# A two-block transformer kernel on one core: dummy products of the identity at stage openings, and a conv FFN whose taps are handed over side by side

## Chip, cores and metric

The kernel runs on one core of a Trainium2 chip. The metric is device time in microseconds (us). Three runs of the kernel before gave 2916.37 to 2916.70 us, median 2916.45.

## The reference

One program computes two stacks of depth 2 on 256 tokens of width 1024, in fp32.

- First stack: an RWKV-7 layer (projections, low-rank gates, the WKV recurrence over 256 steps, group norm, output projection), post-norm, a dense SwiGLU FFN (hidden 2816), post-norm; then causal attention with 16 heads (one MoBA block of 256 keys, so all keys before the query), its output projection, and a mixture of 8 experts of which each token takes 2 (hidden 3584).
- Second stack, on the 256 tokens and 256 context tokens: a layer with neighbourhood attention and a two-way mLSTM side by side, an output projection and a conv FFN on 512 tokens; then multi-head latent attention of the 256 tokens over all 512 keys, its output projection, and a conv FFN on 256 tokens.

The conv FFN is the part whose order changes:

```python
def conv_ffn(h, w_up, conv_w, conv_b, w_down):
    u = dwconv_centred(h @ w_up, conv_w, conv_b)     # 3 taps over the positions, per channel
    a, g = jnp.split(u, 2, axis=-1)
    return (a * jax.nn.silu(g)) @ w_down
```

## The kernel before

The program is a sequence of stages (`K.begin()`), each with a hand-written instruction list for every engine and a barrier between one stage and the next. All weights stream through `weight_ring`, six chunks of 128 x 2048 fp32 (1 MB), loaded by SyncE in the order of a plan; a chunk is loaded as soon as its place is used up (`K.used`).

**Products in two parts.** fp32 accuracy comes from splitting each operand into a rounded part (`high`, fp32r) and the rest (`low`); a product is three fp32r matmuls (high x low, low x high, high x high) that accumulate in PSUM. `class Split` does this for the streamed weights by halves of a chunk (1024 columns): ScalarE (ACT) copies the half into `w_high` (line 265), VectorE (DVE) subtracts it into `w_low` (line 300). In stages that stream x along (`rows`), the same is done for x (`s_x_high` L264, `s_x_low` L298). `depth` 1 keeps two halves, so that a half is split again as soon as PE has used it; `depth` 2 keeps four.

**Openings.** At the start of a stage `act_open` (L275 to L282) splits the first weight half in two pieces, and PE begins with the high x high products of that half (`opening()`: L517 in `linear_rows`, L710 in `gated_ffn`, L386 in `split_cols`, L1860 in `moba_projections`), while DVE makes the first `w_low` and `x_low`. Then PE goes on with the other two parts of the half (L526, L731, L407, L1879).

**gated_ffn.** 11 chunk pairs: for each chunk c a weight chunk for side s=0 (the gated side) and one for s=1, 256 hidden channels each, result in PSUM banks `c % 2 * 4 + s * 2 + h`. Without a convolution ACT applies SiLU to side 0 and DVE multiplies by side 1 (L809). With one, for each c:

- ACT, once both sides are done, writes the centre tap and bias of both (L792, four instructions) and later the SiLU of the chunk before (L767);
- DVE adds the left and right taps of both sides in one go (L832, eight instructions of 128 x 510 in the 512-token FFN), signals `tapped` once, and multiplies the chunk before (L809), before it makes the next `w_low`;
- PE may overwrite the banks of c when `tapped` says that both sides are done. After the last chunk it goes on to the down products (L700), of which the token tiles 0 and 1 take the banks of the last chunk.

The 512-token FFN (depth 1) stands at 2146 to 2530 us of the profile, the 256-token one (depth 2) from 2720 us on.

**WKV.** `wkv` solves triangular systems by levels, two blocks of 128 steps. At its end PE waits for DVE's last masked copy (`dn_at(1,6,1)`, L1578), then makes the last solution (`solved(1, g)`, L1365) and the outputs (`output(1, g)`, L1365 and L1370); DVE copies the outputs (L1595) and normalises them, which ends the stage. PE meanwhile makes conditioning products (L1153).

**attention** (causal, neighbourhood, latent) runs scores (L1724, masks or bias L1731), DVE's maximum (L1801), ACT's exponential (L1820), transposes (L1743), DVE's copy (L1789), the product with v (L1768) and the spreading of sums (L1753), software-pipelined over steps.

**latent** makes the compressed keys and queries of the latent attention, beginning with 64 matmuls (L3531).

`K.ident` is the 128 x 128 identity in fp32, used for transposes. PSUM bank 7 is `K.ps[7]`.

Of the kernel before, what the change touches and what calls it, by code (L numbers as in the profile page):

```python
# [21 lines left out]
P = 128  # L22
D = 1024
KT = D // P
T = 256
TT = T // P
# [339 lines left out]
def split_cols(K, x, jobs, late, parts_at, x_at, extra, kept, small):  # L366
# [11 lines left out]
    with K.begin() as block:  # L378
        @block.tensor
        def _(pe):  # L380
            def opening():
                for h in range(2):
                    for k in range(KT // 2):
                        if h == 0 and k % 2 == 0:
                            pe.wait_ge(*xsplit.at(k // 2 + 1))
                        nc.tensor.matmul(bank(0, h), parts.hi[:, 0, k * 256 + h * P:k * 256 + h * P + P],  # L386
                                         xhi[:, k, :], start=(k == 0), stop=False)

            extra.tensor(pe, 0)
            for c in range(chunks):  # L390
                if c == 1:
                    extra.tensor(pe, extra.pairs)
                if c >= 3:
                    pe.wait_ge(*evac.at(c - 2))
                for i in range(2):
                    opened = c == i == 0
                    if opened:
                        opening()
                    pe.wait_ge(*parts.low.at(2 * c + i + 1))
                    for h in range(2):  # L400
                        for k in range(KT // 2):
                            j = i * (KT // 2) + k
                            if c == h == 0 and j % 2 == 0:
                                pe.wait_ge(*xlow.at(j // 2 + 1))
                            at = slice(k * 256 + h * P, k * 256 + h * P + P)
                            for p, (ws, xs) in enumerate(((parts.lo, xhi), (parts.hi, xlo), (parts.hi, xhi))[0:2 if opened else 3]):
                                last = nc.tensor.matmul(bank(c, h), ws[:, i, at], xs[:, j, :],  # L407
                                                        start=(j == 0 and p == 0 and not opened), stop=(j == KT - 1 and p == 2))
                    last.then_inc(*(K.used if i else parts.half).up())
                K.taken += 1  # L410
# [63 lines left out]

def last_steps(tts, depth):

# [14 lines left out]
def linear_rows(K, x, kts, evac, tts=TT, after=None, sqrts=None, root_bufs=(), depth=2, loads=(), tail=None):  # L492
# [4 lines left out]
    chunks = len(kts) // 2  # L497
    opened = K.begun["opened"]
    opened.base = opened.n
    with ExitStack() as st:  # L500
# [4 lines left out]
        with K.begin() as block:  # L505
            @block.tensor
            def _(pe):
                if not depth:
                    mm_rows(K, pe, x, kts, banks=tuple(range(8)), tts=tts)
                    return  # L510
                def opening():
                    pe.wait_ge(*opened.at(1))
# [142 lines left out]
def gated_ffn(K, x, hid, chunks, over, tail, conv=None, late=None, base=0):  # L655
# [18 lines left out]
    with ExitStack() as st:  # L674
# [13 lines left out]

        read = tapped if conv else free
        with K.begin() as block:  # L690
            @block.tensor
            def _(pe):
# [12 lines left out]
                def opening():  # L705
                    for h in range(2):
                        for k in range(KT // 2):
                            if h == 0 and k % 2 == 0:
                                pe.wait_ge(*xsplit.at(k // 2 + 1))
                            nc.tensor.matmul(bank(0, 0, h), parts.hi[:, 0, k * 256 + h * P:k * 256 + h * P + P],  # L710
                                             xhi[:, k, :], start=(k == 0), stop=False)

                for c in range(chunks):
                    if c >= 2:
                        pe.wait_ge(*read.at(c - 1))
                    for s in range(2):
                        for i in range(2):
                            opened = c == s == i == 0
# [16 lines left out]
                early = range(2, tts) if tts > TT else range(tts)  # L735
                pe.wait_ge(*read.at(chunks - 1))
                for i in range(2):
# [4 lines left out]
                if tts > TT:  # L742
                    pe.wait_ge(*read.at(chunks))
                    for i in range(2):
                        products(0, i, range(TT)).then_inc(*(K.used if i else parts.half).up())
                K.taken += 1
# [11 lines left out]
                K.taken += 1  # L758
                pe.wait_ge(*read.at(chunks))
                tail[0](pe)  # L760

            @block.scalar
            def _(act):
                def silu(c):
                    act.wait_ge(*tapped.at(c + 1))
                    for h in range(2):
                        last = nc.scalar.activation(side[:, c % 2, 0, h, :], side[:, c % 2, 0, h, :], ACT.Silu)  # L767
                    last.then_inc(*gated.up())
# [7 lines left out]
                for c in range(chunks):  # L776
                    parts.act(act, 2 * c + 1 if conv else 2 * c)
                    if conv is None:
                        act.wait_ge(*K.used.at(2 * c + 1))
                        if c >= 2:  # L780
# [4 lines left out]
                        continue  # L785
                    act.wait_ge(*K.used.at(2 * c + 2))
                    if c >= 2:
                        act.wait_ge(*free.at(c - 1))
                    for s in range(2):
                        for h in range(2):  # L790
                            j = (chunks * 2 if s == 0 else 0) + 2 * c + h
                            last = nc.scalar.activation(side[:, c % 2, s, h, :], bank(c, s, h), ACT.Identity,  # L792
                                                        bias=conv[1][:, j:j + 1], scale=conv[0][:, j, 1:2])
                    last.then_inc(*centre.up())
                    if c >= 1:
                        silu(c - 1)
                if conv is not None:
                    silu(chunks - 1)
                for c in range(down):
# [4 lines left out]
            def _(dve):  # L804
# [12 lines left out]
                for c in range(chunks):  # L817
                    parts.dve(dve, 2 * c + 1 if conv or c < chunks - 1 else 2 * c)
                    if conv is None:
                        dve.wait_ge(*K.used.at(2 * c + 2))  # L820
                        product(c)
                        if late and 1 <= c < 5:
                            late(dve, c - 1)
                        continue
                    dve.wait_ge(*centre.at(c + 1))
                    for tap, (dst, src) in enumerate(((slice(1, T), slice(0, T - 1)), (slice(0, T - 1), slice(1, T)))):
                        for s in range(2):
                            for h in range(2):
# [4 lines left out]
                                                                      ALU.mult, ALU.add)  # L833
                        K.v(dve, last, tapped if tap else None)
                    if c >= 1:
                        product(c - 1)
                if conv is not None:
                    product(chunks - 1)
                for c in range(down):
# [472 lines left out]
def wkv(K, AR, Bt, Kt, vr, G0, G1, G2, G3, Dm, DTs, Wm, tri, level, Brow, Krow, Sbd, dstate, bones, yr, gr, bonus, gg, gb, small):  # L1312
# [27 lines left out]
    with K.begin() as block:  # L1340
        @block.tensor
        def _(pe):
# [101 lines left out]
            for c in range(2):  # L1444
# [30 lines left out]
                for g in range(2):  # L1475
# [5 lines left out]
                    up(last, "d_made")  # L1481
                filler(c, 6, 0)
            pe.wait_ge(*dn_at(1, 6, 1))
            for g in range(2):
# [203 lines left out]
def attention(K, st, units, outs, room=None):  # L1688
# [26 lines left out]
    with K.begin() as block:  # L1715
        @block.tensor
        def _(pe):
# [39 lines left out]
            def apply(s):  # L1757
# [12 lines left out]
                last.then_inc(*applied.up())  # L1770

            for s in range(NS + 3):
                if s < NS:
# [62 lines left out]
def moba_projections(K, x, jobs, vr, late, rounded):  # L1836
# [9 lines left out]
    with ExitStack() as st:  # L1846
# [5 lines left out]
        with K.begin() as block:  # L1852
            @block.tensor
            def _(pe):
                def opening():
                    for h in range(2):
                        for k in range(KT // 2):
                            if h == 0 and k % 2 == 0:
                                pe.wait_ge(*xsplit.at(k // 2 + 1))
                            nc.tensor.matmul(bank(0, h), parts.hi[:, 0, k * 256 + h * P:k * 256 + h * P + P],  # L1860
                                             xhi[:, k, :], start=(k == 0), stop=False)

                for c in range(wide):
                    if c >= 3:
# [1605 lines left out]
def latent(K, st, hT, wkv, wq, ups, ckvT, cqT, kT, qT, vr, H, QK):  # L3470
# [34 lines left out]
    with K.begin() as block:  # L3505
        @block.tensor
        def _(pe):
# [14 lines left out]
            def values(n):  # L3522
# [3 lines left out]
                                 start=True, stop=True).then_inc(*value.up())  # L3526

            pe.wait_ge(*K.load.now())
            for tt in range(4):
# [401 lines left out]
```

## Time and profile before

| | us |
|---|---|
| median of 3 runs | 2916.45 |
| the profiled execution, its own time | 2922.09 |
| its span, first to last instruction | 2920.3 |
| TensorE (PE) busy | 2767.4 (95%) |
| VectorE (DVE) busy | 1863.6 (64%) |
| ScalarE (ACT) busy | 1470.4 (50%) |
| mean granted TensorE clock | 0.960 of full speed |

### The profile page before, as it was taken

Reading aid. Unit: us, or ns where it says so; the run is one execution under the profiler, and the core shown is the slowest. Engines: PE = TensorE matmul, PEld = TensorE weight load, DVE = VectorE, ACT = ScalarE, POOL = GpSimd, SP = SyncE. Lnnn points to the kernel's source line nnn. Section 1 sums busy time; section 2 is a strip of 40 time slices with the busy share of each in tenths; the row PEclk is TensorE's granted clock in tenths of the full one; section 3 lists DMA queues with packets and bytes.
Section 4 is the critical chain, followed back from the end, with each engine's and each line's share of the span. In section 5 each row is a group of like instructions: output and inputs, shape, how many; then the busy total and the mean of one; then the engine's idle time right before and its main releaser. Section 6 shows DMA issues by size and latency. Waiting matters only on the chain. (4 is left out here: it accounts for less than half of the span.)

```text
span 2920.3 us, 40440 instructions
## 1 busy us (share of the span) xinstructions
PE 2767.4 (95%) x16411; PEld 2296.0 (79%) x16411; DVE 1863.6 (64%) x2196; ACT 1470.4 (50%) x1908; POOL 17.6 (1%) x42
## 2 busy tenths in 40 slices
PE   7989899999899999999999999999889999899898
PEld 5688699787788888888888877868677777746897
DVE  4555555545888889888898872345454453445676
ACT  4142444444676777767776753333443332443554
POOL 0000000000100000000000000000000000000000
PEclk9998899988999999999999999899899999999999
DMA  5400655744999999989999988321022222201343
GB/s 188 144 2 2 248 187 187 266 153 180 378 353 349 368 361 360 363 343 368 351 367 366 363 331 211 101 73 44 34 77 87 101 88 87 97 27 31 142 177 113
DMA packets 105508, 588.87 MB, mean 202 GB/s; under 512 B 31264, under 2 KB 32336, under 8 KB 35952
## 3 DMA queue, kind: packets, MB, share of 16 engines
q1 hardware_dynamic: 104176, 584.43, 54.1%
q8 instruction: 132, 2.16, 0.3%
q10 hardware_dynamic: 1152, 1.88, 0.2%
q14 instruction: 48, 0.39, 0.0%
HBM read 585.20 MB, written 1.07 MB: 201 GB/s over the span
## 5 line engine op out<-in xcount | busy, mean ns | idle before, releaser
L2456 DVE TENSOR_TENSOR s_w_low<-weight_ring,s_w_high 128x2048 fp32r<-128x2048 f32 x336 | 759.5, 2290 | 103.9 <-ACT s_w_high L2396 103.9
L2396 ACT ACTIVATE s_w_high<-weight_ring 128x2048 fp32r<-128x2048 f32 x336 | 630.4, 1910 | 97.9 <-PE bank L2378 72.6
L2378 PE MATMUL bank<-s_w_high,s_tokens 128*128 128x512 f32 x1792 | 565.8, 391 | 7.4 <-POOL s_tokens L2535 7.4
L300 DVE TENSOR_TENSOR s_w_low<-weight_ring,s_w_high 128x1024 fp32r<-128x1024 f32 x254 | 309.1, 1222 | 223.7 <-ACT s_w_high L265 209.6
L265 ACT ACTIVATE s_w_high<-weight_ring 128x1024 fp32r<-128x1024 f32 x246 | 258.5, 1053 | 305.5 <-PE bank L731 272.6
L2378 PEld LDWEIGHTS bank<-s_w_high,s_tokens 128*128 128x128 f32 x1792 | 337.5, 188 | 77.7 <-POOL s_tokens L2535 7.5
L2378 PE MATMUL bank<-s_w_low,s_tokens 128*128 128x512 f32 x896 | 349.5, 390 | 0.0
L731 PE MATMUL bank<-s_x_high,s_w_low 128*128 128x256 f32 (+1 forms) x1056 | 340.1, 322 | 8.7 <-DVE s_w_low L300 8.2
L731 PE MATMUL bank<-s_x_low,s_w_high 128*128 128x256 f32 (+1 forms) x1056 | 338.6, 321 | 0.0
L731 PE MATMUL bank<-s_x_high,s_w_high 128*128 128x256 f32 (+1 forms) x1032 | 328.7, 318 | 0.0
L731 PEld LDWEIGHTS bank<-s_x_high,s_w_low 128*128 128x128 f32 x1056 | 203.9, 193 | 26.6 <-DVE s_w_low L300 12.0
L731 PEld LDWEIGHTS bank<-s_x_low,s_w_high 128*128 128x128 f32 x1056 | 203.8, 193 | 13.5
L731 PEld LDWEIGHTS bank<-s_x_high,s_w_high 128*128 128x128 f32 x1032 | 196.8, 191 | 13.5
L2378 PEld LDWEIGHTS bank<-s_w_low,s_tokens 128*128 128x128 f32 x896 | 168.9, 188 | 34.8
L2360 PE MATMUL bank<-s_w_high,s_hidden_low 128*128 128x512 f32 x448 | 179.4, 400 | 0.0
L2360 PE MATMUL bank<-s_w_high,s_hidden_high 128*128 128x512 f32 x448 | 175.4, 392 | 0.0
L2360 PE MATMUL bank<-s_w_low,s_hidden_high 128*128 128x512 f32 x448 | 174.3, 389 | 0.0
L700 PE MATMUL bank<-s_w_high,s_hidden 128*128 128x512 f32 x528 | 163.9, 390 | 5.0 <-DVE s L832 3.3
L700 PEld LDWEIGHTS bank<-s_w_high,s_hidden 128*128 128x128 f32 x528 | 99.1, 188 | 27.0 <-DVE s L832 3.7
L832 DVE SCALAR_TENSOR_TENSOR s<-bank,s,s 128x510 f32<-128x510 f32 (+1 forms) x176 | 96.2, 610 | 22.3 <-ACT s L792 21.6
L700 PE MATMUL bank<-s_w_low,s_hidden 128*128 128x512 f32 x264 | 102.8, 389 | 0.0
L2360 PEld LDWEIGHTS bank<-s_w_high,s_hidden_high 128*128 128x128 f32 x448 | 84.1, 188 | 18.6
(528 smaller groups left out, 4161.8 us busy)
## 6 DMA issues: line engine op xcount, KB each, us to landing
weight_ring<-moe_w SPq DMA_DIRECT2D x336, 1024.0 KB, 7.0
weight_ring<-ada_w SPq DMA_DIRECT2D x48, 1024.0 KB, 7.3
weight_ring<-ffn_up SPq DMA_DIRECT2D x44, 1024.0 KB, 4.8
weight_ring<-ffn_w_in SPq DMA_DIRECT2D x22, 1024.0 KB, 4.9
weight_ring<-ffn_down SPq DMA_DIRECT2D x22, 1024.0 KB, 4.8
weight_ring<-ffn_w_down SPq DMA_DIRECT2D x11, 1024.0 KB, 4.8
weight_ring<-w_rkv_cols SPq DMA_DIRECT2D x8, 1024.0 KB, 14.9
weight_ring<-moba_qk SPq DMA_DIRECT2D x8, 1024.0 KB, 12.1
```

What stands on the lines that cost most here:

```text
L265: K.nc.scalar.activation(self.hi[:, b, :], self.source(c, i), ACT.Copy).then_inc(*self.high.up())
L300: K.nc.vector.tensor_tensor(self.lo[:, b, :], self.source(c, i), self.hi[:, b, :], ALU.subtract)\
L700: last = nc.tensor.matmul(K.ps[base + tt * 2 + h][:, :], xs[:, b, t], ws[:, b, n], start=(c == 0 and i == 0 and p == 0), stop=(c == down - ...
L731: last = nc.tensor.matmul(bank(c, s, h), ws[:, b, at], xs[:, j, :], start=(j == 0 and p == 0 and not opened), stop=(j == KT - 1 and p == 2))
L832: last = nc.vector.scalar_tensor_tensor(o, i, conv[0][:, j, 2 * tap:2 * tap + 1], o, ALU.mult, ALU.add)
L2360: last = nc.tensor.matmul(K.ps[2 + h][:, :], xs[:, step % 2, k, :], ws[:, b, c], start=(s == 0 and k == 0 and m == 0), stop=(s == WIDE - 1 ...
L2378: last = nc.tensor.matmul(o[:, :], both[:, e % 2, xs, k, :], ws[:, b, c], start=(k == 0 and m == 0), stop=(k == KT - 1 and m == 2))
L2396: nc.scalar.activation(halves(whi, kind, n, i), raw(kind, n, i), ACT.Copy).then_inc(S["high"].h, 1)
L2456: V.tensor_tensor(halves(wlo, kind, n, i), raw(kind, n, i), halves(whi, kind, n, i), ALU.subtract)\
```

## The change

A helper issues n products of the identity with itself into bank 7, with no semaphore and no reader:

```diff
+def idle_products(K, n=6):
+    for _ in range(n):
+        K.nc.tensor.matmul(K.ps[7][:, 0:P], K.ident[:, :], K.ident[:, :], start=True, stop=True)
```

It is called in PE's list as its first instructions (n = 6) of `linear_rows` (when depth is not 0: four stages), `gated_ffn` (three), `attention` (three) and `moba_projections` (one); in `split_cols` behind the first conditioning products (`extra.tensor(pe, 0)`); and with n = 5 in `latent`, ahead of its wait for small loads, and in `wkv`:

```diff
                 filler(c, 6, 0)
+            idle_products(K, 5)
             pe.wait_ge(*dn_at(1, 6, 1))
...
+            idle_products(K, 5)
             pe.wait_ge(*K.load.now())
```

In `gated_ffn` with a convolution the two sides of a chunk are handed over separately. `tapped` and `centre` now count sides, two for each chunk:

```diff
-        read = tapped if conv else free
+        def read(pe, c, s):
+            pe.wait_ge(*(tapped.at(2 * c + s + 1) if conv else free.at(c + 1)))
...
                 for c in range(chunks):
-                    if c >= 2:
-                        pe.wait_ge(*read.at(c - 1))
                     for s in range(2):
+                        if c >= 2 and (conv or s == 0):
+                            read(pe, c - 2, s)
...
                 if tts > TT:
-                    pe.wait_ge(*read.at(chunks))
                     for i in range(2):
-                        products(0, i, range(TT)).then_inc(*(K.used if i else parts.half).up())
+                        for tt in range(TT):
+                            if i == 0:
+                                read(pe, chunks - 1, tt)
+                            last = products(0, i, [tt])
+                        last.then_inc(*(K.used if i else parts.half).up())
```

in ACT's list:

```diff
-                    parts.act(act, 2 * c + 1 if conv else 2 * c)
...
-                    act.wait_ge(*K.used.at(2 * c + 2))
-                    if c >= 2:
-                        act.wait_ge(*free.at(c - 1))
                     for s in range(2):
+                        parts.act(act, 2 * c + s)
+                        act.wait_ge(*K.used.at(2 * c + s + 1))
+                        if c >= 2 and s == 0:
+                            act.wait_ge(*free.at(c - 1))
                         for h in range(2):
...
-                    last.then_inc(*centre.up())
-                    if c >= 1:
-                        silu(c - 1)
-                if conv is not None:
-                    silu(chunks - 1)
+                        last.then_inc(*centre.up())
+                    silu(c)
```

in DVE's list:

```diff
-                    dve.wait_ge(*centre.at(c + 1))
-                    for tap, (dst, src) in enumerate(((slice(1, T), slice(0, T - 1)), (slice(0, T - 1), slice(1, T)))):
-                        for s in range(2):
+                    for s in range(2):
+                        parts.dve(dve, 2 * c + s)
+                        dve.wait_ge(*centre.at(2 * c + s + 1))
+                        for tap, (dst, src) in enumerate(((slice(1, T), slice(0, T - 1)), (slice(0, T - 1), slice(1, T)))):
                             for h in range(2):
...
-                        K.v(dve, last, tapped if tap else None)
-                    if c >= 1:
-                        product(c - 1)
-                if conv is not None:
-                    product(chunks - 1)
+                            K.v(dve, last, tapped if tap else None)
+                    product(c)
```

So the SiLU and the product of a chunk follow its own taps and no longer those of the next chunk.

## Rows read from the trace of the kernel before

**Rows 1.** The page, busy times and granted clock in 40 slices.
```profile
PE 2767.4 (95%) x16411; PEld 2296.0 (79%) x16411; DVE 1863.6 (64%) x2196; ACT 1470.4 (50%) x1908; POOL 17.6 (1%) x42
...
PEclk9998899988999999999999999899899999999999
```
**Rows 2.** Windows: stretch and length, busy of PE, PEld, DVE, ACT, POOL; clock, DMA.
```profile
265.69:299.82 34.13, 31.83 (x182) 30.58 (x182) 11.27 (x15) 1.77 (x3) 0.00 (x0) 0.50 0.00 0
...
357.85:364.67 6.82, 6.55 (x29) 6.21 (x30) 6.38 (x8) 5.09 (x8) 0.00 (x0) 0.50 1.00 419
...
641.15:658.22 17.07, 17.07 (x78) 11.88 (x78) 7.23 (x16) 8.32 (x40) 0.00 (x0) 0.50 0.16 10
...
2057.69:2085.00 27.31, 14.34 (x44) 11.20 (x43) 14.55 (x54) 14.35 (x43) 0.00 (x0) 0.50 0.00 0
...
2678.91:2685.74 6.83, 6.05 (x14) 4.79 (x15) 2.97 (x5) 1.75 (x3) 0.00 (x0) 0.50 0.00 0
```
**Rows 3.** Timeline of PE in WKV: start, us, what [idle before, releaser].
```profile
226.70 3.68 PE L1365 MATMUL bank<-s 128*128 128x64 f32 x32
...
246.97 1.11 PE L1370 MATMUL bank<-s,s 128*128 128x128 f32 x8
...
274.11 7.06 PE L1365 MATMUL bank<-s 128*128 128x64 f32 x32 [1.52 <-DVE s L1578]
281.95 7.09 PE L1365 MATMUL bank<-s 128*128 128x64 f32 x32 [0.78 <-DVE s L1591]
288.83 2.02 PE L1370 MATMUL bank<-s,s 128*128 128x128 f32 x8
...
297.37 2.02 PE L1370 MATMUL bank<-s,s 128*128 128x128 f32 x8
```
**Rows 4.** Timeline of DVE, end of WKV and opening of the first FFN.
```profile
299.43 0.69 DVE L1595 COPY x<-bank 128x512 f32<-128x512 f32 x1 [7.77 <-PE bank L1370]
...
361.83 3.49 DVE L300 TENSOR_TENSOR s_w_low<-weight_ring,s_w_high 128x1024 fp32r<-128x1024 f32 x3
```
**Rows 5.** Timeline of PE, causal attention and start of latent attention.
```profile
639.14 0.49 PE L1724 MATMUL bank<-s,s 64*128 64x128 f32 x4 [1.97 <-PEq L1852]
...
655.57 1.93 PE L1743 MATMUL bank<-ident,s 128*128 128x128 f32 x8
...
660.74 1.06 PE L1743 MATMUL bank<-ident,s 128*128 128x128 f32 x8
...
2610.71 0.67 PE L1724 MATMUL bank<-s,s 96*128 96x512 f32 x1 [1.38 <-PEq L3505]
```
**Rows 6.** Timeline of PE, one tile of products with a diagonal, at either clock.
```profile
2129.17 3.64 PE L2769 MATMUL bank<-s,x 128*128 128x128 f32 x16 [3.60 <-DVE s L2853]
2133.10 2.05 PE L2769 MATMUL bank<-s,x 128*128 128x128 f32 x16 [0.29 <-DVE s L2853]
```
**Rows 7.** Timeline of PE in the 512-token FFN.
```profile
2206.21 0.50 PE L731 MATMUL bank<-s_x_high,s_w_low 128*128 128x512 f32 x1 [0.92 <-DVE s_w_low L300]
...
2229.18 0.50 PE L731 MATMUL bank<-s_x_high,s_w_low 128*128 128x512 f32 x1 [0.91 <-DVE s_w_low L300]
...
2411.09 0.50 PE L700 MATMUL bank<-s_w_high,s_hidden 128*128 128x512 f32 x1 [3.29 <-DVE s L832]
```
**Rows 8.** Timeline of DVE in the 512-token FFN.
```profile
2198.22 5.47 DVE L832 SCALAR_TENSOR_TENSOR s<-bank,s,s 128x510 f32<-128x510 f32 x8 [1.45 <-ACT s L792]
2203.73 1.29 DVE L809 TENSOR_TENSOR s<-s 128x512 f32<-128x512 f32 x2
2204.94 1.22 DVE L300 TENSOR_TENSOR s_w_low<-weight_ring,s_w_high 128x1024 fp32r<-128x1024 f32 x1
```
**Rows 9.** Timeline of ACT in the 512-token FFN.
```profile
2194.46 1.06 ACT L265 ACTIVATE s_w_high<-weight_ring 128x1024 fp32r<-128x1024 f32 x1 [4.32 <-PE bank L731]
2195.42 2.77 ACT L792 ACTIVATE s<-bank,s,s 128x512 f32<-128x512 f32 x4
```
**Rows 10.** Window of the latent attention.
```profile
2610.71:2675.20 64.49, 64.46 (x512) 42.84 (x512) 43.87 (x71) 26.91 (x69) 0.00 (x0) 1.00 0.00 1
```

More of the change, by code:

```diff
@@ L389, in _ @@
             extra.tensor(pe, 0)
+            idle_products(K)
             for c in range(chunks):
@@ L510, in _ @@
                     return
+                idle_products(K)
                 def opening():
@@ L711, in opening @@
                                              xhi[:, k, :], start=(k == 0), stop=False)
+                idle_products(K)
                 for c in range(chunks):
-                    if c >= 2:
-                        pe.wait_ge(*read.at(c - 1))
                     for s in range(2):
+                        if c >= 2 and (conv or s == 0):
+                            read(pe, c - 2, s)
                         for i in range(2):
@@ L735, in _ @@
                 early = range(2, tts) if tts > TT else range(tts)
-                pe.wait_ge(*read.at(chunks - 1))
+                read(pe, chunks - 2, 1)
                 for i in range(2):
@@ L758, in _ @@
                 K.taken += 1
-                pe.wait_ge(*read.at(chunks))
+                read(pe, chunks - 1, 1)
                 tail[0](pe)
@@ L764, in silu @@
                 def silu(c):
-                    act.wait_ge(*tapped.at(c + 1))
+                    act.wait_ge(*tapped.at(2 * c + 1))
                     for h in range(2):
@@ L776, in _ @@
                 for c in range(chunks):
-                    parts.act(act, 2 * c + 1 if conv else 2 * c)
                     if conv is None:
+                        parts.act(act, 2 * c)
                         act.wait_ge(*K.used.at(2 * c + 1))
@@ L817, in _ @@
                 for c in range(chunks):
-                    parts.dve(dve, 2 * c + 1 if conv or c < chunks - 1 else 2 * c)
                     if conv is None:
+                        parts.dve(dve, 2 * c + 1 if c < chunks - 1 else 2 * c)
                         dve.wait_ge(*K.used.at(2 * c + 2))
@@ L1770, in apply @@
                 last.then_inc(*applied.up())
+            idle_products(K)
             for s in range(NS + 3):
@@ L1861, in opening @@
                                              xhi[:, k, :], start=(k == 0), stop=False)
+                idle_products(K)
                 for c in range(wide):
```

## Prediction, written before the result was known

> **What bounds the kernel now.** I read the page first: TensorE (PE) is busy 95% of the span, and its granted clock, mean 0.960, dips in many slices [rows 1]. The chain of waits says little (it stops at 2720 us), so I went on to the stretches in which the clock is at its lower level, 1.2 GHz instead of 2.4. With two levels, a mean of 0.960 means 8% of the span, some 230 us, at the lower one; five of the stretches stand in [rows 2], the other openings below repeat their pattern. The reader is to see two things there: most of them begin at or near the opening of a stage, and PE is busy in most of their time, so in them PE does its work at half speed and usually sets the end. Next the time lines of PE and DVE at the stages the change touches [rows 3 to 5, 7 to 9], last the rows that price a product [rows 6].
>
> **Price of a product.** One idle product is an fp32 128x128 matmul, which this trace records as two instructions (L2769: one product for each two records). Twelve instructions cost 12/16 of 2.05 us = 1.5 us at the high level and 12/16 of 3.64 = 2.7 us at the low one [rows 6]; five products 1.3 and 2.3 us.
>
> **Taps by side.** This is the part I am surest of. In the context-and-latent FFN (512 tokens) DVE does the eight taps of a chunk and the previous product as one block, 5.47 + 1.29 us, and only then the w_low that PE waits for: it starts at 2204.94 and ends at 2206.16, PE starts at 2206.21 [rows 7, 8]. Without the wait PE's matmuls start 0.228 us apart, here 1.30, so 1.07 us are lost, and that returns every 22.97 us, nine times: 9.6 us. With sides apart the longest block is four taps and a product, 2.74 + 1.29 = 4.0 us. It begins 2.5 us after the weight chunk is used up (w_high 1.06, centre taps half of 2.77, [rows 9]), ends at 6.5 to 7, and the w_low that it could delay can't start before PE's next half is done (24 x 0.228 = 5.47 us) and split by ACT (1.06), so at 6.6, and PE wants it at 10.9. The slack is over 2 us, so all nine waits go. At the turn to the down products PE waited for all taps of the last chunk, 3.29 us by the row [rows 7]; now tile 0 needs the first side alone, and the second side's taps (about 2.7 us from 2404.7) end before six matmuls of tile 0 are through (2408.9). PE restarts at 2407.5 instead of 2411.09: 3.5 us. What is late next is the w_low there (0.8 us before, the same after), which I leave. In the 256-token FFN no PE wait names the taps: nothing. Sum 13.1; bounds 8 (the waits move to ACT's order and half remain) and 15.
>
> **The WKV stage's last wait.** PE waits 1.52 us for DVE before 274.11, and runs L1365 and L1370 at the low level until 299.8, almost without a pause; DVE's normalisation, which ends the stage, hangs on the last product [rows 3, 4]. Five products there take 2.3 us instead of the wait, so by themselves they make everything 0.8 us later. What they can bring is the clock. L1365 keeps PE busy with 64 columns to a 128-wide weight load, and the clock stayed low through it; L1370's 128 columns (2.02 us at 297.37) came just before it rose [rows 3]. If it rises behind the products, at about 276, the rest goes by the rows at the high level: L1365 x32 3.68 us (3.6 to the next start) instead of 6.9, L1370 x8 about 0.95 instead of 1.9. From 274.9: 1.0 us at the low level, 3.1, the wait for DVE 0.8, then twice 3.6 + 0.95, which ends at 288.9 instead of 299.3. Gain 10.4 us; bounds -0.8 and 11. I take 10.4, because the products are the densest work there is (columns and weights of 128, no wait between), but it is no sure thing: the same 2.02 us of L1370 at 288.83 did not raise the clock, those at 297.37 did. The difference can only be where they fell.
> The Trainium skill ("TensorE: Matmul & The Clock Gate", "What's actually happening") says that the window in which activity is judged is "free-running", not started by the kernel's work. The trace agrees with its two L1370 stretches. By that rule a stretch of this length can miss, and the sum would lack 11.2 us; that is a rival below.
>
> **Causal attention.** PE starts here at once (idle only for the barrier, 1.97 us, [rows 5]), so six products delay it by 1.5 us at the high level. The clock fell 2 us into the stage, and stayed low for 17.07 us with PE busy in all of them [rows 2, 5]. With dense products right behind the 1.97 us gap I expect it not to fall. The same transposes took 1.93 us low and 1.06 high [rows 5]; at that ratio the 17.07 us become 9.4, of which the fill of the pipeline (score, maximum, exponential, only then transposes) gives back about 1.2. Net of the 1.5: 5 us. Bounds -2.7 and 6.
>
> **Other openings where PE waits anyway** (four row projections, three FFNs, the MoBA projections; the split columns at 1764, where the clock is up again when the real work starts, nothing). PE is idle there, since ACT must first split weights and x, so the products cost nothing at the high level. They save low clock, but not half of it, because DVE is late next. Worked for the first FFN: at the high level the opened half ends at 361.95 instead of 363.65; the second half needs the w_low that DVE makes from 361.83 on (the three of [rows 4], 3.49 us, the first ready at 363.0), and ends at 365.85 instead of 366.9: 1.0 of the 6.82 us. In the projection at 2678.91 [rows 2] the first half frees its buffer at 2681.5 instead of 2683.6, the split behind it takes 3.1, and the next chunk starts at 2684.9 instead of 2687.2: 2.2 us. In the same way 0.9 (318), 1.5 (563), 1.6 (682, 3.4 us of low clock, no row), 1.0 (2079), 0.8 (2146), 0.75 (2723): 9.75 in all with the two worked ones. Some will find the clock down all the same; I take 8. Bounds: -3 (products at the low level end 0.4 to 1.3 us after the opening could start, hidden by DVE in most) and 22, half of PE's busy time in these stretches.
>
> **Openings where PE has work at once.** Neighbourhood attention (1950.72), latent attention (2610.71, 1.38 us after its last work, [rows 5]) and the latent stage (2548.50) start on the barrier. Real work there is as dense as the products, so these buy no clock and cost their time: 1.5 + 1.5 + 1.3 = 4.3 us, at the low level up to 7.7; bounds -7.7 and +2.
>
> **Sum.** 13.1 + 10.4 + 5 + 8 - 4.3 = 32.2 us. The profiled execution took 2922.09 us (span 2920.3 and 1.8 around it), 5.6 above the median of the runs, 2916.45; I take the sum from the median: **2884 us**. All later openings shift against the places where the clock changes, and stages without products (27 us of low clock before 2085, [rows 2]) may gain or lose a few us; I give that +-5 and no mean.
>
> **Rivals.**
> A, the clock misses in WKV: everything else as above, 2884 + 11.2 = 2895. For it: L1370 at 288.83, and 34 us of low clock with PE busy. Against it: nothing else in the stretch is as dense.
> B, causal attention falls all the same (or the taps' waits only move): 5 turns into about -2, 2891. For it: its own fill is thin, pairs of 64-row matmuls.
> C, the clock does not answer to these products anywhere, their operand being mostly zeros or their time too short: taps 13.1, products -0.8 - 2.7 - 5 - 2, so 2.6 faster: 2914, no measurable change.
> D, the other side: the changed shift makes the clock fall at the opening of latent attention, and its rate of busy PE is not enough to raise it again, as in the causal one. That stage is 64.49 us with PE busy throughout [rows 10]; all of it at half speed is at most +64, at the causal ratio of 1.8 about +50. From about 33 us on it outweighs everything else: 2884 + 50 = 2934. Against it: the gap before it is only 1.38 us, and it runs at the high level now.
>
> **How the numbers follow.** My forecast 0.55 (own range 2876 to 2891), A 0.22, B 0.14, C 0.06, D 0.03. A difference under 0.2% (5.8 us) can't be told from none. Faster: forecast, A and B with a small part lost, 0.92; same 0.05 (C); slower 0.03 (D). The range for 8 in 10 reaches from 2873 to the upper edge of A, 2902.
>
> **What would show it.** In the profile after: no 0.9 us idle of PE at L731 behind DVE w_low in the 512-token FFN and its chunk period 21.9 instead of 22.97; the idle before L700 behind the taps gone; the clock at 1.00 from about 276 to the end of the WKV products, L1365 x32 in 3.7 instead of 7 us; the causal attention without its 17 us of low clock; L1724's first start 1.5 us after the barrier in the two other attentions. I am wrong if L1365 still takes 7 us, if the low stretches stand at the openings as before, or if PE still waits for DVE at every chunk of the FFN.

## The result, and the profile after

| | before | after |
|---|---|---|
| median of the comparison, 20 runs each | 2910.24 us (2901.06 to 2921.98) | 2892.89 us (2881.20 to 2901.99) |
| ratio after/before, 95% interval | | 0.9942 [0.9928, 0.9955] |
| profiled execution, own time | 2922.09 | 2893.41 |
| its span | 2920.3 | 2891.6 |
| PE busy | 2767.4 (95%) | 2764.5 (96%) |
| mean granted clock in it | 0.960 | 0.970 |

The kernel became 17.35 us faster where 32.2 were forecast: 2892.89 against 2884, inside the range (2873 to 2902), outside the forecast's own one (2876 to 2891). Luck helped this number. With 20 runs the kernel before has a median of 2910.24, not 2916.45, so the sum started 6.2 us too high, and that hid a part of the 14.9 us of gain that did not come. And the profiled execution of before, from which all durations came, took longer than any of the 20.

A ratio here and below compares all runs of a kernel with those of the kernel before that were timed beside them, so it is not quite the quotient of the two medians; "by the ratio" means its distance from 1 times 2909 us.

First the page of the kernel after: PE, and its clock in 40 slices.

```profile
PE 2764.5 (96%) x16575; PEld 2302.8 (80%) x16575; DVE 1866.4 (65%) x2196; ACT 1471.1 (51%) x1908; POOL 27.5 (1%) x42
...
PEclk9999899998999999999999999899899999999999
```

The clock's row looks almost as in [rows 1]; some dips have moved or changed. So the parts have to be read from windows and time lines. The windows of the kernel after (stretch and length, busy of PE, PEld, DVE, ACT, POOL with counts; clock, DMA share, GB/s) are: the WKV stage from its five products on, the causal attention's opening, and most of the 512-token FFN.

```profile
268.04:292.12 24.08, 23.08 (x140) 21.88 (x142) 9.26 (x11) 0.00 (x0) 0.00 (x0) 0.65 0.00 1
...
627.08:655.00 27.92, 27.01 (x251) 20.40 (x253) 16.07 (x35) 15.96 (x67) 0.00 (x0) 1.00 0.17 33
...
2150.00:2380.00 230.00, 230.00 (x1017) 190.46 (x1016) 123.91 (x147) 85.48 (x108) 0.00 (x0) 1.00 0.26 96
```

The FFN: PE has no idle left in 230 us. What it waits for at the turn and behind it is in the time lines of the kernel after (start, us, engine, line, what, [idle before, releaser]), PE first, then DVE:

```profile
2382.93 0.50 PE L710 MATMUL bank<-s_w_high,s_hidden 128*128 128x512 f32 x1 [0.81 <-DVE s_w_low L300]
2392.25 0.50 PE L710 MATMUL bank<-s_w_high,s_hidden 128*128 128x512 f32 x1 [0.86 <-DVE s_w_low L300]
```
```profile
2186.03 2.84 DVE L845 SCALAR_TENSOR_TENSOR s<-bank,s,s 128x510 f32<-128x510 f32 x4
2188.90 1.29 DVE L821 TENSOR_TENSOR s<-s 128x512 f32<-128x512 f32 x2
2190.19 1.23 DVE L300 TENSOR_TENSOR s_w_low<-weight_ring,s_w_high 128x1024 fp32r<-128x1024 f32 x1
```

These answer to [rows 7, 8]: four taps and the product, 4.1 us, then w_low, and PE no longer waits for it; the two waits that stay at the turn's w_low were there before (0.82 and 0.86), and the one of 3.29 us for the taps is gone.

The WKV stage's end, PE after, answers to [rows 3]:

```profile
268.04 1.38 PE L480 MATMUL bank<-ident 128*128 128x128 f32 x10
269.64 3.76 PE L1375 MATMUL bank<-s 128*128 128x64 f32 x32 [0.22 <-DVE s L1589]
274.17 6.36 PE L1375 MATMUL bank<-s 128*128 128x64 f32 x32 [0.78 <-DVE s L1602]
280.32 2.02 PE L1380 MATMUL bank<-s,s 128*128 128x128 f32 x8
282.14 6.93 PE L1375 MATMUL bank<-s 128*128 128x64 f32 x32
288.86 2.02 PE L1380 MATMUL bank<-s,s 128*128 128x128 f32 x8
```

Here the forecast failed. The clock was at its high level when the products ran (1.38 us for ten instructions) and for the first 32 of what is L1365 before (3.76 us); at 275.0 it fell and stayed low over the rest, until 292.1. The products did not bring it up, since it was up; it stayed up for 32 matmuls more than in [rows 3], and then it fell all the same. Nor are [rows 2] and [rows 3] a case of a fall at this wait: their stretch begins at 265.69, some 7 us ahead of the place where the products stand.

The causal attention after (PE) answers to [rows 5]: six products, 1.5 us, and all of it at the high level.

```profile
627.08 1.57 PE L480 MATMUL bank<-ident 128*128 128x128 f32 x12 [1.97 <-PEq L1864]
628.58 0.49 PE L1735 MATMUL bank<-s,s 64*128 64x128 f32 x4
```

The two profiled executions differ by 28.7 us, 11 more than the medians. Followed along PE's instructions, after leads by 11.1 us where the 512-token FFN's L731 (L742 after) begins, by 21.8 behind its last chunk and by 25.1 at the first instruction behind its down products: 14.1 in this stage, and nothing else in the trace is as large or as steady. Of the rest, 4.9 us came in the end of WKV and 5.6 over the causal attention, from ahead of its opening to behind it. It led by 3.6 us before the first product of the change was reached, and lost 4.5 between 705 and 1743 us, where the change puts nothing.

### The profile page after: what moved, and what is told of

It is laid out like the page before. It is cut to its first block and busy times, and to the rows that moved or that the text cites. A ratio compares the mean times of both kernels' runs of the same rounds, so it can differ in the third digit from the quotient of the medians.

```text
span 2891.6 us, 40808 instructions
## 1 busy us (share of the span) xinstructions
PE 2764.5 (96%) x16575; PEld 2302.8 (80%) x16575; DVE 1866.4 (65%) x2196; ACT 1471.1 (51%) x1908; POOL 27.5 (1%) x42
## 5 line engine op out<-in xcount | busy, mean ns | idle before, releaser
L742 PE MATMUL bank<-s_x_high,s_w_low 128*128 128x256 f32 (+1 forms) x1056 | 336.7, 319 | 1.5 <-DVE s_w_low L300 1.0
L742 PE MATMUL bank<-s_x_low,s_w_high 128*128 128x256 f32 (+1 forms) x1056 | 336.1, 319 | 0.0
L742 PE MATMUL bank<-s_x_high,s_w_high 128*128 128x256 f32 (+1 forms) x1032 | 328.6, 318 | 0.0
L742 PEld LDWEIGHTS bank<-s_x_high,s_w_low 128*128 128x128 f32 x1056 | 201.8, 191 | 16.6 <-DVE s_w_low L300 1.7
L742 PEld LDWEIGHTS bank<-s_x_low,s_w_high 128*128 128x128 f32 x1056 | 201.8, 191 | 13.5
L742 PEld LDWEIGHTS bank<-s_x_high,s_w_high 128*128 128x128 f32 x1032 | 196.7, 191 | 13.5
```

The lines of the kernel that those rows point to most:

```text
L742: last = nc.tensor.matmul(bank(c, s, h), ws[:, b, at], xs[:, j, :], start=(j == 0 and p == 0 and not opened), stop=(j == KT - 1 and p == 2))
```

## The experiments

The main question was why 17 us came where 32 were forecast: whether the products' gain in clock was sized from one unlucky execution, and which part is worth what. The theories, in their numbers, stand in each expectation. Each kernel below was timed against the kernel before. "Products" are the calls of idle_products.

**The kernel before again, and the whole change again**

No edit.

> The kernel before, unchanged, profiled a second time. Theory 1 (the low-clock stretches at stage openings fall by chance from execution to execution, and the profile that the forecast rested on was an unlucky one): times spread over some 10 us, and this profile has other low stretches than the first; the WKV stage's end no longer has 34 us of them, its span is nearer 2908 than 2920. Theory 2 (the stretches are fixed by the program): the same stretches at the same places within 2 us, span 2920.

> The changed kernel, unchanged, profiled a second time. Both: ratio 0.994. Theory 1: other low-clock stretches than in its first profile at the stages that run near the limit (end of WKV, the stage after the expert FFN, mLSTM), but none in causal attention; the FFN period of 21.9 us is the same. Theory 2: the same stretches as in its first profile.

Measured: before 2909.01 us median, ratio 0.9997 [0.998, 1.0015]. After 2890.48, ratio 0.9919 [0.9898, 0.994]. The 12 executions of the unchanged kernel lie between 2900.5 and 2922.6. The second trace of before is the find (PE, end of WKV):

```profile
271.41 5.38 PE L1365 MATMUL bank<-s 128*128 128x64 f32 x32 [1.52 <-DVE s L1578]
277.57 7.09 PE L1365 MATMUL bank<-s 128*128 128x64 f32 x32 [0.78 <-DVE s L1591]
284.45 2.02 PE L1370 MATMUL bank<-s,s 128*128 128x128 f32 x8
286.27 3.99 PE L1365 MATMUL bank<-s 128*128 128x64 f32 x32
290.10 1.11 PE L1370 MATMUL bank<-s,s 128*128 128x128 f32 x8
```

Against [rows 3] the same program with the same wait has 13.7 us of low clock there (273.3 to 287.0), not 34.1, and is through at 291.1, 8.2 us earlier than in the first trace; 6.4 of them come from the last 16 matmuls ahead of the wait on. That is more than half of the 10.4 us that I had written down for the five products, and it came by itself. The low clock of the whole trace adds up to 198.5 us, against 233.2 the first time. Most stretches stand at the same stages again, so it is their lengths more than their places that differ: WKV's end alone makes 20 of the 35 us. The two traces of the whole change agree there, with 17.1 us from 275.0 and from 276.7 (178.1 and 164.7 us in all): at this place theory 2 fits them.

**One part alone**

```diff
 taps_only: after.py, without any call of idle_products
 products_only: after.py, with gated_ffn's waits, taps and order as before
```

> The change without any idle product: taps by side alone. Theory 1: it carries most of the gain, 12 to 14 us faster than before, ratio 0.9955; in the 512-token FFN the chunk period is 21.9 us and PE's waits for DVE are gone. Theory 2 (the products carry the gain, the FFN's waits only moved): under 4 us, ratio above 0.9985.

> All idle products, the gated FFN in the order of before (no taps by side). Theory 1: 4 us faster than before, 1 to 7, ratio 0.9986: gains at causal attention and the openings less the cost of products that PE must do ahead of work. Theory 2: 15 to 19 us faster, ratio 0.9945.

Measured: taps only 2899.42 us, 0.9956 [0.9939, 0.9973], 12.8 us faster. Products only 2906.22 us, 0.9992 [0.9975, 1.0009], no change that can be told. The waits of PE in the 512-token FFN with the products only (line, releaser: total us, times, longest):

```profile
PE bank L740 <- DVE s_w_low L300: 8.2, 9, 0.9
PE bank L708 <- DVE s L841: 3.3, 1, 3.3
PE bank L708 <- DVE s_w_low L300: 1.5, 2, 0.8
```

and with the taps only:

```profile
PE bank L708 <- DVE s_w_low L300: 1.7, 2, 0.9
```

So the first term stands, mechanism and size. All 14 traces show it, without a single exception: from PE's first L731 in the 512-token FFN to its last down product it is 374.7, 375.6 and 376.4 us (start to start, worked out from the records) in the three with the old order, and 359.3 to 360.3 in the eleven with the sides apart; a chunk pair takes 22.97 us in the former and 21.76 in the latter. Something that the forecast did not have goes with it: in two of the three with the old order (before again, products only) a stretch of 3.4 us of low clock begins about 1 us behind the end of the wait of 3.29 us, and in none of the eleven.

And the products do win clock: the mean granted clock over all runs is 0.9647 for before (12 runs), 0.9640 for the taps alone (11), 0.9709 for the products alone (12) and 0.9706 for the whole change (20). Two levels make 0.0062 more of 2908 us into 36 us less at the low one, worth up to 18 us where PE is never idle. The products as a whole brought about 2 (0.0008 of 2909). What do they cost?

I measured in each trace the time from the start of PE's last instruction before an opening to the start of its first real one behind it (worked out from the records, start to start, us):

| opening | before again | after | tripled |
|---|---|---|---|
| projection at 311 | 2.72 | 4.31 | 7.73 |
| first FFN, 350 | 2.72 | 4.12 | 7.04 |
| MoBA projections, 554 | 2.17 | 2.33 | 6.63 |
| causal attention, 629 | 2.36 | 3.87 | 8.17 |
| projection at 663 | 2.62 | 2.99 | 5.67 |
| neighbourhood attention, 1939 | 3.93 | 6.27 | 9.74 |
| projection at 2071 | 4.98 | 6.35 | 9.68 |
| 512-token FFN, 2138 | 3.93 | 3.94 | 6.35 |
| latent stage, 2523 | 2.34 | 3.52 | 5.76 |
| latent attention, 2585 | 1.65 | 3.07 | 5.74 |
| all 14, these, WKV and three more, against before again | 0 | +12.4 | +54.4 |

The forecast had these at 6.6: 1.5 in the causal attention, 4.3 where PE has work at once, 0.8 in WKV (where they in fact cost nothing: 1.80 after, 1.79 before) and nothing where PE waits anyway. That last is wrong. At the projection the products begin 1.33 us after the barrier, not at once, and ScalarE is done after 2.30; PE of the kernel before in its second trace, and of the kernel after:

```profile
303.55 3.65 PE L593 MATMUL bank<-ident,x 128*128 128x128 f32 x16 [3.43 <-PEq L1340]
309.50 1.25 PE L517 MATMUL bank<-s_w_high,s_x_high 128*128 128x512 f32 x4 [2.30 <-ACT s_w_high L277]
```
```profile
303.22 3.65 PE L601 MATMUL bank<-ident,x 128*128 128x128 f32 x16 [3.43 <-PEq L1350]
308.20 2.90 PE L480 MATMUL bank<-ident 128*128 128x128 f32 x12 [1.33 <-PEq L595]
310.76 1.63 PE L525 MATMUL bank<-s_w_high,s_x_high 128*128 128x512 f32 x3
```

At the low level they last 2.90 us, so the projection starts 1.6 us late; at the high one still 0.4 (663). At most 18 us for less low clock, less 12.4 if all delays at the openings reach the end, leaves 5.6. That is an estimate and not a bound, since a delay can hide behind a later wait.

**Where in the change the products matter**

```diff
 causal_only
+if room is None:       # the causal attention alone
+    idle_products(K)
 openings_only: calls in row projections, FFNs and MoBA projections kept, the other three taken out
 wkv_none: the one call ahead of WKV's last wait taken out
 lean: no products at the two other attentions and the latent stage
```

> Taps by side, and of the products only the six ahead of the causal attention. Theory 1 (where a stretch of low clock lands differs from one execution to the next in most places, but the causal attention's returns in every trace without products, 17.1, 17.1 and 6.8 + 3.4 us, and in none with them; that is the products' only worth): about 5 us faster than with the taps alone, so 18 us faster than before, ratio 0.994; no low clock from the attention's opening to its end. Theory 2 (the earlier products change where the stretch falls, not those at the attention itself): low clock in the attention as with the taps alone, ratio 0.9956.

> Taps by side, and of the products those at the openings of projections and FFNs, where PE waits for the split weights anyway; none in WKV, the attentions and the latent stage. Theory 1 (these are worth nothing): as the taps alone, 0.9956, with 17 or so us of low clock in the causal attention. Theory 2 (they bring the 8 us of the forecast): 0.993. By either, PE's first product after the opening comes as early as before.

> The whole change without its five products at the last wait of the WKV stage. Theory 1 (they bring nothing and cost 0 to 0.8 us): within 1 us of the whole change, 13.7 to 17.1 us of low clock from about 273. Theory 2 (they bring part of the 10.4 us of the forecast): 3 us or more slower than the whole change, and a stretch of 20 us or more.

> The whole change without the products where PE has work at once: none at the neighbourhood and the latent attention and the latent stage. Theory 1 (there they only cost their time): 1.5 + 1.5 + 1.3 = 4.3 us faster than the whole change, ratio about 0.992; low clock in neither of these stages, as in the traces of the taps alone. Theory 2 (they keep the clock from falling there, as in the causal attention): 17 us of low clock at one of the three openings, and no gain or a loss of up to 7 us.

Measured: causal only 2891.69 us, 0.9947 [0.9929, 0.9965]; openings only 2887.06, 0.9936 [0.9916, 0.9957]; no WKV products 2898.98, 0.9967 [0.9952, 0.9983]; lean 2891.55, 0.9934 [0.9912, 0.9955]. All but one lie between the taps alone (0.9956) and the two measurements of the whole change (0.9942, 0.9919). Causal only had no low clock in the attention, as its theory 1 says, but its time lies between those of the two theories (0.994, 0.9956). Openings only had 20.5 us of low clock in the causal attention, about what its theory 1 had, and a ratio next to its theory 2 (0.993); against the taps alone that is 5.8 us faster, uncertain by 8, so neither nothing nor the forecast's 8 us is ruled out. "As early as before" was a miss: its openings start 3.4 us later in all. The one that stands out is the kernel without WKV's products: slower than the whole change and than openings only, which has none there either, with intervals that hardly touch. That is what its theory 2 has for the time (3 us or more), but the stretch in its trace is shorter than either theory says. If the five products were the cause, openings only should be slow too. Its trace has this (PE, end of WKV, then the causal attention's opening; then the window of the latter):

```profile
275.98 3.76 PE L1375 MATMUL bank<-s 128*128 128x64 f32 x32 [1.52 <-DVE s L1588]
280.52 5.35 PE L1375 MATMUL bank<-s 128*128 128x64 f32 x32 [0.78 <-DVE s L1601]
285.67 2.02 PE L1380 MATMUL bank<-s,s 128*128 128x128 f32 x8
287.48 4.55 PE L1375 MATMUL bank<-s 128*128 128x64 f32 x32
...
629.64 2.01 PE L480 MATMUL bank<-ident 128*128 128x128 f32 x12 [1.97 <-PEq L1863]
631.58 0.80 PE L1734 MATMUL bank<-s,s 64*128 64x128 f32 x4
```
```profile
630.62:654.51 23.89, 23.89 (x118) 17.24 (x116) 7.94 (x18) 9.34 (x42) 0.00 (x0) 0.50 0.16 24
```

Two readings fall here. WKV's end had only 6.8 us of low clock with no products at all. And the causal attention fell to the low level for 23.9 us although its six products ran: the clock dropped in the middle of them (2.01 us instead of 1.57). Until then I had taken it as shown that they hold it there. Counted over all 14 traces, the low clock in the causal attention was 17.1, 17.1, 6.8 and 20.5 us in the four without products there, and with them 0 in seven, 3.4 in the one with three times as many, and 23.9 in two. By these counts they make the fall less likely; they don't prevent it. The lean kernel has the same 3.4 us of low clock at the neighbourhood attention's opening as the taps alone, and opens there and in the latent ones 2.3, 1.2 and 1.4 us sooner than the whole change: its 4.9 us are gained, but the time, 3 us lower by the means of all runs (2889.6 against 2892.6), can't tell them.

**More of it**

```diff
 wkv_ten, lean_ten (the latter on lean)
-idle_products(K, 5)    # WKV
+idle_products(K, 10)
 tripled: 18 for 6, 15 for 5, everywhere
 filled: lean_ten, and in the mLSTM stage's end
 flip(1)
+idle_products(K, 10, 1)   # into bank 1
 flip(2)
 pe.wait_ge(*mixed.at(8))
+idle_products(K, 8, 3)
 flip(3)
```

> The whole change, with ten products instead of five at the last wait of the WKV stage. Theory 1 (the stretch of low clock at the end of that stage begins at 273 to 277 us whatever is done at the wait, and lasts 14 us or more): 1.3 to 2.3 us slower than the whole change, ratio about 0.9945 if that is 0.9935; low clock from about 275 for 14 to 34 us. Theory 2 (five were too few for the clock to rise): the stretch shrinks to under 7 us, L1365 x32 takes 3.7 us, and 2 to 4 us are gained against the whole change in spite of the products.

> The same, with ten products instead of five at the last wait of the WKV stage. Theory 1 (that the one trace with ten had 6.8 us of low clock behind them was chance): 13.7 us or more of low clock there, and as much as without, or 1.3 us more. Theory 2 (ten are enough to shorten it): 6.8 us again, L1365 and L1370 through by about 290 (with five 290.8, minus what the longer wait costs), 1 to 3 us faster than with five; ratio 0.991.

> The whole change with three times as many products at each place (18 and 15). Theory 1 (products buy clock in the causal attention alone, and cost their time where PE has work at once): three stages of attention 3.0 us each, the latent stage 2.5, WKV 2.5 to 3.5, and at the ten or so other openings what is left of 4.5 us after PE's wait there, 0 to 1.5 each: 14 to 30 us slower than the whole change, ratio 0.998 to 1.004. Theory 2 (more products win more clock): the total of low clock falls below 120 us from 163 to 176, and the loss stays under 8 us.

> As the second kernel, with ten more products in PE's wait of 6 us for ScalarE ahead of a transpose of the mLSTM stage's end, and eight in the next. In every trace so far the clock is low for 17 to 27 us from about 2050, over the opening of the projection behind it. Theory 1 (the clock comes up when PE's waits are filled): that stretch shrinks to under 10 us, the opening's eight matmuls take 1.9 instead of 3.6 us, 2 to 4 us faster than the second kernel. Theory 2 (the place is given by other things): as the second kernel, within 1.5 us.

Measured: WKV ten 2886.59 us, 0.9932 [0.9907, 0.9957]; lean ten 2887.09, 0.991 [0.9886, 0.9934]; tripled 2918.56, 1.0041 [1.0025, 1.0056]; filled 2886.85, 0.9928 [0.9908, 0.9948].

Tripled prices the products: 0.0099 of 2909 us, 29 us slower than the change (25 by the means of all runs), at the same mean clock (0.9709 over 12 runs). The openings' delays grew by 42 us in the table, so a part of them did not reach the end; behind which waits it hid was not followed. Three times as many products win no more clock, and a set of them costs 13 to 15 us. Theory 1 there, 14 to 30, holds.

For WKV all 14 traces stand side by side (start to start, worked out from the records: from the 16 matmuls ahead of the last wait to the first one behind the stage's products; and the duration of the first 32 of L1365):

| products | stage's end, us | first 32, us |
|---|---|---|
| none (before, before again, taps, causal, openings, no WKV) | 28.8, 22.4, 23.9, 22.4, 22.4, 19.6 | 7.06, 5.38, 7.06, 5.52, 5.35, 3.76 |
| five (after, again, products, lean) | 23.9, 23.85, 24.15, 22.7 | 3.76 in each |
| ten (ten, lean ten, filled) | 20.3 in each | 3.68 in each |
| fifteen (tripled) | 24.1 | 3.68 |

The clock does answer here: without products the first 32 behind the wait of 1.52 us are at the low level in whole or in part in five of six traces, with products in none of eight. But the fall only moves on, to behind the next wait, 0.78 us: the mean without products is 23.3 us, with five 23.6. With ten the stretch is short, 6.8 us, in all three.

Why a later fall gains nothing stands in where the clock rises again. In all 14 traces it rises 0.1 to 1.6 us behind the end of one of the two L1370 blocks of this stage. In three traces of four that have no products and no low clock between 150 and 265 us it falls at 270.9 to 273.3 and rises behind the first block: 22.4 us each (the fourth is the first trace of before, 28.8). The three with five products that came to it in the same way fall at 275.0 to 276.7, pass the first block at the low level, and rise only behind the second: 23.9, 23.85 and 24.15 us. There five products cost 1.5 us, by these few traces.

The window and PE's lines of the kernel with ten in WKV:

```profile
279.35:286.18 6.83, 6.83 (x35) 6.83 (x34) 1.34 (x2) 0.00 (x0) 0.00 (x0) 0.50 0.00 0
```
```profile
271.28 2.50 PE L480 MATMUL bank<-ident 128*128 128x128 f32 x20
273.62 3.68 PE L1375 MATMUL bank<-s 128*128 128x64 f32 x32
278.08 5.90 PE L1375 MATMUL bank<-s 128*128 128x64 f32 x32 [0.79 <-DVE s L1602]
```

Two more sets of traces can be compared in this way. Those of the taps alone, of lean and of ten in WKV all have a stretch of 3.4 us at 207.7 to 208.0, ahead of the changed call, and so came to it alike: none, five and ten then took 23.9, 22.7 and 20.3 us. Lean ten and the kernel without WKV's products are alike too (3.4 us at 149.3, 6.8 at 163): ten and none took 20.3 and 19.6, and both fell for 23.9 us at 630.6. I call such a list of low stretches ahead of the stage's end the course of an execution. Ten products are worth 3.6 us in the one course and cost 0.7 in the other, by one trace each; what sets the course was not tested. By the times, ten and five can't be told apart (0.9932 against 0.9942 and 0.9919; 0.991 against 0.9934).

Filled did what it should to the clock: the stretch at about 2050, 17.1 to 27.3 us in all other traces, became one of 6.8 us, with another of 6.8 that begins 17 us ahead of it (PE, then the window):

```profile
2037.07 3.04 PE L480 MATMUL bank<-ident 128*128 128x128 f32 x20
2041.62 0.66 PE L3318 MATMUL bank<-ident,s 128*128 128x128 f32 x4 [1.51 <-ACT s L3452]
2042.12 1.95 PE L480 MATMUL bank<-ident 128*128 128x128 f32 x16
2046.71 0.65 PE L3318 MATMUL bank<-ident,s 128*128 128x128 f32 x4 [2.64 <-ACT s L3452]
...
2053.81 2.86 PE L525 MATMUL bank<-s_w_high,s_x_high 128*128 128x512 f32 x8
```
```profile
2048.60:2055.40 6.80, 4.14 (x16) 3.88 (x17) 2.45 (x4) 5.29 (x14) 0.00 (x0) 0.50 0.00 0
```

and it was worth nothing that shows, since PE waits there for ScalarE and the stage ends when ScalarE does. Its expectation of 2 to 4 us was a miss. No version is shown to be better than the change; lean ten has the lowest ratio, and its interval overlaps that of the change run again.

## Why the prediction was right and where it was wrong

- **Taps by side, 13.1.** Right in mechanism and size. 12.8 us by the ratio of the kernel with the taps alone (7.9 to 17.7 by its interval), 14.1 in the stage in the traces. The nine waits and the one of 3.29 us are gone, and no other took their place. The chunk period fell to 21.76 us where 21.9 was forecast.
- **WKV's last wait, 10.4.** The failed step: "If it rises behind the products, at about 276". It took a clock that was low behind the wait in one trace for what this place does, and overlooked that in this trace the stretch had begun some 7 us ahead of the products' place [rows 2]. In the trace after it was high there, and in three of the six traces without products it was high for a part of the 32 and in one for all, so there was less to raise; what went with the products was a fall put off to the second 32, and a rise put off as well. The 10.4 us measured 4.9 between the two traces compared, which differ by chance there too, and by the means of all traces they are a loss of 0.4 (23.25 us without, 23.65 with five). Of the rivals A is the nearest: its 2895 is 2.1 us off, though by the same luck with the start, for from 2910.24 it would be 2889. The probability of 0.22 was too low because I took one execution's 34.1 us as the normal case, when a second one of the same kernel shows 13.7. The Trainium skill ("TensorE: Matmul & The Clock Gate", "What's actually happening") calls the window in which activity is judged "free-running". I had cited that sentence for one stretch and drawn nothing from it for the others, whose lengths can differ from one execution to the next. The traces agree: before shows 34.1 and 13.7 us at WKV's end, with no edit between them.
- **Causal attention, 5.** Right in the trace compared (no low clock, 1.5 us of delay, 5.6 us gained net). As a mean over executions it is less: it fell in two of the ten traces with products there, and one had a little.
- **Other openings, 8.** Wrong in the price, open in the gain. The products cost 0.0 to 1.6 us at each instead of nothing (5.9 us over these in the trace after, 3.4 in that of openings only). By the time of openings only they are worth 5.8 us, uncertain by 8. No run settles it.
- **Openings where PE has work at once, -4.3.** Right: -4.9 in the table.
- **The sum.** All products were forecast at +19.1 net, and measured at about 2 alone (0.9992) and 4 and 11 on top of the taps (0.9942 and 0.9919 against 0.9956), each uncertain by 5 to 8. Their delays were 12.4 us, forecast 6.6; their clock 36 us, worth at most half of that.
- **Median and execution.** The sum was taken from the median of three runs within 0.4 us of each other; the 20 of the comparison have 2910.24. That three agree so closely said nothing about the spread of the kernel, about 6 us as a standard deviation.

Rival D did not come up: latent attention ran at the high level in all traces. Rival C is nearly what the time of the products alone says (no measurable change), but not for its reason: the clock does answer, by 36 us. Rival B's fall came in two of the ten traces with products there, not in the one compared.

What stays open: how often an execution takes which course through WKV, so what five or ten products are worth there on the average, and why the kernel without them is 7 us slower than the change by the means of its runs (2899.6 against 2892.6), while openings only is 3 faster. That was not tested.

## What to carry to other kernels

A wait that returns at each chunk, with the engine that it waits for half idle, can be counted from one trace, and here its gain came in all eleven traces; stretches of low clock can't, since the next execution of the same program may have them much shorter or longer: take two or three traces of the unchanged kernel before sizing them. Filler products belong only where they end, even at the low level, before the real work could start. The time from the last instruction before the barrier to the first real one behind it, compared in both traces, is the most that they cost.

## What was not expected of the hardware

- One unchanged program on one core spreads over 22 us (2900.5 to 2922.6 in 12 runs), and its mean granted clock from 0.968 to 0.960 with it.
- At WKV's end the clock rose behind an L1370 block in all 14 traces, 0.1 to 1.6 us behind its end, as the prediction had read it in [rows 3] from one. In eight of them that is the first block, and the rise then falls among the next 32 of L1365 (4.55 us without WKV's products, 3.99 in the second trace of before, against 6.93 at the low level in the trace after); in the other six it is the second, and the first had passed without it.
- PE was busy in all of 23.89 us at the low level in the causal attention (the window above), and the clock did not rise in that time.
- 36 us less of low clock in an execution came with no measurable gain of time, since the products that won it delay the work at the openings.
